# Feed-forward down projections on one Trainium2 core: eight block products of two k groups done as seven, shared ones added to the residual by VectorE

## What is computed

```python
def swiglu_2(x, w_in, w_out):                     # w_in 1024 x 5632, w_out 2816 x 1024
    gate, up = jnp.split(x @ w_in, 2, axis=-1)
    return (jax.nn.silu(gate) * up) @ w_out

def second_block(x, ...):
    h = x
    for i in range(2):
        h = layer_norm(DN_ALPHA * h + 0.5 * swiglu_2(h, ffn_w_in[i, 0], ffn_w_out[i, 0]), ...)   # a0, b0
        m = gla_mixer(h, ...) if i == 0 else retention_mixer(h, ...)
        h = layer_norm(DN_ALPHA * h + m, ...)
        h = layer_norm(DN_ALPHA * h + 0.5 * swiglu_2(h, ffn_w_in[i, 1], ffn_w_out[i, 1]), ...)   # a1, b1
    return h
```

## Time and profile before

| | |
|---|---|
| runs | median 1592.44 us (1590.9 to 1592.71, three runs) |
| the profiled execution | 1591.92 us, its span 1590.1 us |
| mean granted TensorE clock | 0.999 of full |
| TensorE matmul busy | 1580.2 us, 99% of the span |
| VectorE busy | 1118.8 us, 70% |
| ScalarE busy | 866.0 us, 54% |
| DMA | 341 MB, 215 GB/s on average |

### The profile page before, as it was taken

The page is one execution under the profiler, slowest core; times in us unless marked ns, Lnnn a source line. Parts: engine busy times, 40 slices in busy tenths (PEclk is TensorE's granted clock), DMA queues, the critical chain, the costliest instruction groups (busy, mean ns, idle before and its releaser), DMA issues.

```text
span 1590.1 us, 18691 instructions
## 1 busy us (share of the span) xinstructions
PE 1580.2 (99%) x7659; PEld 1317.9 (83%) x7659; DVE 1118.8 (70%) x1081; ACT 866.0 (54%) x907; POOL 105.0 (7%) x126
## 2 busy tenths in 40 slices
PE   9999999999999999999999999999999999999998
PEld 6888897788888888888988888888888998888886
DVE  6785566677875678865668886678856657688964
ACT  7564457556653766642655665366543435456650
POOL 0141000000000000001010000000000131000000
PEclk9999999999999999999999999999999999999999
DMA  8874463467854687562648765578545544587750
GB/s 339 247 237 190 179 245 133 159 252 231 282 181 172 263 280 265 177 240 96 238 159 310 232 225 213 224 229 287 211 185 196 192 172 152 189 292 233 242 212 27
DMA packets 51892, 341.38 MB, mean 215 GB/s; under 512 B 6240, under 2 KB 6624, under 8 KB 13408
## 3 DMA queue, kind: packets, MB, share of 16 engines
q1 hardware_dynamic: 44000, 301.94, 50.7%
q0 software_dynamic: 7584, 38.12, 10.8%
q10 hardware_dynamic: 224, 0.14, 0.0%
HBM read 339.12 MB, written 1.05 MB: 214 GB/s over the span
## 4 chain that ended last, share of the span: by engine, by line
PE 96%; DVE 2%; DMA 1%; ACT 1%; issue 0%; SPq 0%; DVEq 0%; ACTq 0%
PE bank L833 24%; PE bank L846 24%; PE bank L837 21%; PE bank L895 4%; PE bank L897 4%; PE bank L900 4%; PE bank L783 3%; PE bank L850 3%; PE bank L932 1%; PE bank L931 1%; PE bank L929 1%; DVE split L1876 1%; DMA h<-in_x 0%; DMA whole<-in_w_gla 0%; PE bank L1318 0%; PE bank L1108 0%
## 5 line engine op out<-in xcount | busy, mean ns | idle before, releaser
L1876 DVE TENSOR_TENSOR split<-whole,split 128x2048 fp32r<-128x2048 f32 (+2 forms) x329 | 704.4, 2161 | 203.8 <-ACT split L1436 202.1
L1436 ACT ACTIVATE split<-whole 128x2048 fp32r<-128x2048 f32 (+1 forms) x313 | 581.7, 1876 | 265.2 <-DVE whole L1880 38.7
L833 PE MATMUL bank<-split,xh 128*128 128x512 f32 x1052 | 288.1, 396 | 0.0
L846 PE MATMUL bank<-split,xh 128*128 128x512 f32 x1052 | 282.1, 390 | 0.0
L837 PE MATMUL bank<-split,xl 128*128 128x512 f32 x880 | 235.8, 390 | 0.0
L846 PEld LDWEIGHTS bank<-split,xh 128*128 128x128 f32 x1052 | 197.2, 188 | 41.8 <-DVE split L1876 0.4
L833 PEld LDWEIGHTS bank<-split,xh 128*128 128x128 f32 x1052 | 192.9, 188 | 40.7 <-issue 2.8
L837 PEld LDWEIGHTS bank<-split,xl 128*128 128x128 f32 x880 | 165.2, 188 | 35.4
L833 PE MATMUL bank<-split,th 128*128 128x512 f32 x524 | 143.7, 392 | 0.0
L837 PE MATMUL bank<-split,tl 128*128 128x512 f32 x524 | 142.2, 389 | 0.0
L846 PE MATMUL bank<-split,th 128*128 128x512 f32 x524 | 142.1, 389 | 0.0
(11 more groups left out here) (312 smaller groups left out, 1727.0 us busy)
## 6 DMA issues: line engine op xcount, KB each, us to landing
whole<-in_w_a_gate_up SPq DMA_DIRECT2D x48, 1024.0 KB, 7.4
whole<-in_w_b_gate_up SPq DMA_DIRECT2D x48, 1024.0 KB, 7.1
whole<-in_w_f_gate_up SPq DMA_DIRECT2D x45, 1024.0 KB, 7.1
whole<-in_w_ret SPq DMA_DIRECT2D x24, 1024.0 KB, 4.9
whole<-in_w_f_down SPq DMA_DIRECT2D x20, 1024.0 KB, 4.9
whole<-in_w_a_down SPq DMA_DIRECT2D x20, 1024.0 KB, 4.9
whole<-in_w_b_down SPq DMA_DIRECT2D x20, 1024.0 KB, 5.1
whole<-in_w_mix SPq DMA_DIRECT2D x16, 1024.0 KB, 4.9
```

The lines of the kernel that those rows point to most:

```text
L833: pe.matmul(o[:, :], tokens(0, k), whi[:, k, :], start=start and k == 0, stop=False, skip_group_check=True)
L846: ins = pe.matmul(o[:, :], tokens(0, k), wlo[:, k, :], start=False, stop=end, skip_group_check=True)
L1436: act.activation(split[s][:, 0:n], whole[r][:, 0:n], ACT.Copy).then_inc(hi.mark(i), 1)
L1876: dve.tensor_tensor(split[r][:, c0:c1], whole[r][:, c0:c1], split[s][:, c0:c1].bitcast(F32), ALU.subtract).then_inc(lo.mark(*what), 1)
```

## The change

In a0, a1, b0 and b1 the part of the down projection that is groups 2 and 3 (`UNIT_ROWS`) by both column halves and both token halves, eight block products, is done in seven. Their order is `DOWN_UNIT`. Two of the seven go straight into `ACC` (`b22`, `b21`), as does `t4`; `b11`, `t2` and `t3` accumulate one after the other in bank 0, `t1` stands in bank 1, and VectorE adds the state of those banks into the residual `h` each time (six additions, L2343 in the new file). `t2` may accumulate onto bank 0 only once the state after `b11` is added, and `t3` once that after `t2` is. ScalarE copies the transposed blocks of steps 3 to 6 a second time, unrounded, into the `gain` buffer (`ua`); VectorE makes four sums of them in `xn` (`us`) once turn 7 is done, ScalarE their high part in `xh`, VectorE the low part in `xl` (L2380). The gains are loaded only after those sums. The weights `t1` and `t3` get the adding second load, `t2` and `t4` a sum by VectorE (L2000 in the new file). The last four tiles are placed by fixed pairs, no longer the last eight. In GpSimd's queue the adding loads of down stand behind those of gate and up, and ahead of the layer's gains.

```diff
+DOWN_UNIT = (
+    ("tile", 0, 0), ("tile", 0, 1), ("turn", 10), ("blocks",), ("tile", 1, 0),
+    ("product", "b11"), ("product", "t1"), ("product", "b22"), ("product", "t2"), ("tile", 1, 1),
+    ("product", "t3"), ("product", "b21"), ("product", "t4"))
+UNIT_ROWS = (2, 3)
...
@@ plan_ffn
+            for step, *what in DOWN_UNIT:
...
+                    plan(key, {"b11": rows(p, 0), "b21": rows(q, 0), "b22": rows(q, 1),
+                               "t1": rows(p, 1), "t3": rows(p, 1)}.get(m), 4)
+                    if m in ("t1", "t3"):
+                        addend[i] = rows(p, 0) if m == "t1" else rows(q, 1)
...
@@ give_ffn
-            give_blocks(lead, end - 8, among)
-            if into_mixer:
+            give_blocks(lead, end - (4 if name in UNIT_IN else 8), among)
+            if name in UNIT_IN:
+                closing = [[s] for s in slots if into_mixer and s >= 5]
+                give_slots(end - 4, end, closing + [range(5) if into_mixer else slots] * (4 - len(closing)))
+            elif into_mixer:
...
@@ pool_program
-            for g in (7, 8):
-                pool_gain(pool, g)
-            for g in (9,):
-                pool_gain(pool, g)
+            pool_gain(pool, 7)
             pool_sums(pool, "a0")
+            for g in (8, 9):
+                pool_gain(pool, g, "a0")
...
@@ pe_unit
+            def product(m):
+                if m == "b11":
+                    pe.wait_ge(turn_lo.sem, turn_lo.of("t", name, max(range(3, 7), key=order.turned.index)))
+                    pe_product(pe, grp.b11, *block(0, grp.first), bank[0], True)
+                elif m == "t1":
+                    pe.wait_ge(fn.sem, fn.of("ush", name))
+                    pe.wait_ge(vec.sem, vec.of("usl", name))
+                    pe_product(pe, grp.t1, *sums(0), bank[1], True)
+                elif m == "t2":
+                    pe.wait_ge(vec.sem, vec.of("ud", name, 0, 0, "b11"))
+                    pe_product(pe, grp.t2, *sums(1), bank[0], False)
+                elif m == "b22":
+                    pe_product(pe, grp.b22, *sums(3), ACC[0][1], False)
+                elif m == "t3":
+                    pe.wait_ge(vec.sem, vec.of("ud", name, 0, 1, "t2"))
+                    pe_product(pe, grp.t3, *sums(2), bank[0], False)
+                elif m == "b21":
+                    pe_product(pe, grp.b21, *block(0, grp.second), ACC[0][0], False)
+                else:
+                    pe_product(pe, grp.t4, *block(1, grp.second), ACC[1][0], False)
...
@@ act_ffn, turn(j)
+                for m, k in unit_part(name, j):
...
+                    act.activation(ua[:, :, m, k:k + 2, :].rearrange("p t c n -> p c t n"),
...
@@ dve_unit
+            def add(t, n, b, sign, m):
+                hh = half(h[:, t, :], n)
+                dve.wait_ge(passed.sem, passed.of(spot[name + "d", 0, m], 1))
...
+                dve.scalar_tensor_tensor(hh, b[:, :], sign * e.scale / ALPHA, hh, ALU.mult, ALU.add).then_inc(
+                    vec.mark("ud", name, t, n, m), 1)
...
+            def product(m):
+                dve_lows(dve, behind(spot[name + "d", 0, m]))
+                if m == "b11":
+                    add(0, 0, bank[0], 1.0, m)
+                elif m == "t1":
+                    add(0, 1, bank[1], 1.0, m)
+                    add(1, 1, bank[1], 1.0, m)
+                elif m == "t2":
+                    add(0, 1, bank[0], -1.0, m)
+                elif m == "t3":
+                    add(1, 1, bank[0], -1.0, m)
+                    add(1, 0, bank[0], 1.0, m)
```

More of the change, by code:

```diff
@@ L383, in plan_ffn, with rows @@
                             grp.b11 - 0.9, grp.t2 + 0.5, grp.t1 - 0.1, grp.t2 - 0.1)
-            plan_rows(name + "d", A[f"w_{name}_down"], A[f"w_{name}_down_head"])
+            if name not in UNIT_IN:
+                plan_rows(name + "d", A[f"w_{name}_down"], A[f"w_{name}_down_head"])
+                return
+            full, head, key = A[f"w_{name}_down"], A[f"w_{name}_down_head"], name + "d"
+            def rows(g, n):
+                return full[g - 1, n] if g else head[n]
+            p, q = UNIT_ROWS
+            for step, *what in DOWN_UNIT:
+                if step == "tile":
+                    spot[(key, *what)] = len(tiles)
+                    plan(key, rows(*what), 4 if what[0] else 2)
+                elif step == "product":
+                    m, = what
+                    spot[key, 0, m] = i = len(tiles)
+                    product_of[i] = (key, 0, m)
+                    plan(key, {"b11": rows(p, 0), "b21": rows(q, 0), "b22": rows(q, 1),
+                               "t1": rows(p, 1), "t3": rows(p, 1)}.get(m), 4)
+                    if m in ("t1", "t3"):
+                        addend[i] = rows(p, 0) if m == "t1" else rows(q, 1)
+            grp = group[key, 0] = Group(p, q, *(spot[key, 0, m] for m in Group._fields[2:]))
+            load_key[grp.t1], load_key[grp.t3], load_key[grp.b22], load_key[grp.b21] = (
+                grp.b11 - 0.9, grp.t2 + 0.5, grp.t1 - 0.1, grp.t2 - 0.1)
+            for g in (4, 5):
+                for n in range(2):
+                    spot[key, g, n] = len(tiles)
+                    plan(key, rows(g, n), 4)
         w_mix, w_gla, w_ret = A["w_mix"], A["w_gla"], A["w_ret"]
@@ L1034, in pe_ffn @@
             groups = k_groups(22)
-            for g in range(4):
+            if name in UNIT_IN:
+                pe_unit(pe, f, turn)
+                dn = [None] * 8 + [spot[name + "d", g, n] for g in (4, 5) for n in range(2)]
+            for g in range(0 if name in UNIT_IN else 4):
                 for n in range(2):
@@ L1055, in pe_ffn, with pe_unit, block, sums @@
                         pe_pass(pe, dn[8 + n], T, groups[g][0], t, ACC[t][n % 2], False, g == 5)
+        def pe_unit(pe, f, turn):
+            order, name, T = ORDER[f.name], f.name, (f.th, f.tl)
+            groups, grp = k_groups(22), group[f.name + "d", 0]
+            def block(t, g):
+                return [lambda k, m=m: m[:, groups[g][0] + k, t * P:(t + 1) * P] for m in T]
+            def sums(s):
+                return [lambda k, m=m: m[:, s, k, :] for m in (ush, usl)]
+            def tile(g, n):
+                for t in range(2):
+                    if g == 0 and n == 1:
+                        pe.wait_ge(vec.sem, vec.of("mult", name, order.plain[-2], t))
+                    if n == 0 and t == 0:
+                        pe.wait_ge(turn_lo.sem, turn_lo.of("t", name, order.last_turned(2 * g)))
+                    pe_pass(pe, spot[name + "d", g, n], T, groups[g][0], t, ACC[t][n], g == 0, False)
+            def product(m):
[18 more added lines that the diff above has]
+                    pe_product(pe, grp.t4, *block(1, grp.second), ACC[1][0], False)
+            for step, *what in DOWN_UNIT:
+                if step == "tile":
+                    tile(*what)
+                elif step == "turn":
+                    turn(*what)
+                elif step == "product":
+                    product(*what)
         def pe_project(pe):
@@ L1632, in act_ffn @@
                     act.activation(ph[:, :, :], pf[:, :, :], ACT.Copy).then_inc(fn.mark("ph"), 1)
-            act_high(act, ahead(dn[1]))
-            turn(10)
-            act_high(act, dn[11])
+            if name in UNIT_IN:
+                for step, *what in DOWN_UNIT:
+                    if step == "tile":
+                        act_high(act, ahead(spot[(name + "d", *what)], 1))
+                    elif step == "product":
+                        act_high(act, ahead(spot[name + "d", 0, what[0]], 1))
+                    elif step == "turn":
+                        turn(*what)
+                    elif step == "blocks":
+                        act.wait_ge(vec.sem, vec.of("us", name, 3))
+                        act.wait_ge(passed.sem, passed.of(gu[-1], 1))
+                        act.activation(ush[:, :, :, :], us[:, :, :, :], ACT.Copy).then_inc(fn.mark("ush", name), 1)
+            else:
+                act_high(act, ahead(dn[1]))
+                turn(10)
+            act_high(act, dn[-1])
             act_edge(act, e)
```

75 lines of the change are left out of this document (62 added, 13 removed).

## The result

| | before | after |
|---|---|---|
| runs | median 1592.4 us (1590.9 to 1592.71, five) | median 1619.53 us (1616.56 to 1623.75, five) |
| ratio | | 1.0172, 95% interval 1.0161 to 1.0184 |
| the profiled execution | 1591.92 us, span 1590.1 | 1623.75 us, span 1621.9 |
| mean granted clock | 0.999 | 0.991 |

The changed kernel is 27 us slower. The direction and the range (1602 to 1621) hold; the forecast of 1610.5 is 9 us too low. The profiled execution happens to be the slowest of the five, 4.2 us above their median.

The account below looks back on a forecast made before the run. TensorE was taken to bound the kernel: 48 matmuls fewer (-10.9), waits for `b11`'s addition (+13.2), closing tiles (+9.3) and edges (+6.4) gave +18.0 on 1591.9; with the median 0.5 higher, 1610.5 us, range 1602 to 1621.

Parts of the forecast that it names:

- What bounds the kernel: TensorE multiplies in 99% of the span, so each matmul less saves its full spacing and each added wait costs its length.
- Work beside other work at nothing: Per layer, added ScalarE copies and splits, two adding loads on GpSimd and one load on SyncE were costed at nothing.
- The margin before D: D is a0's first down matmul after turn 7, at 678.57; `t1`'s adding load was to end about 2 us ahead.
- The wait for `b11`'s addition: Before `t2` in all four layers, TensorE waits 3.3 us for VectorE's queue: +13.2 us, up to +16.4.
- The closing tile and the edge: In a0 and b0, 4.6 us for the late closing load (+9.3) and 3.2 us before transposing `h` (+6.4).
- the clock falls: Rival: TensorE drops to the lower clock after each of eight waits, 1.6 us each, 13 in all: 1623; chance 0.10.
- the rivals within 0.2%: Closing loads in time, so only `b11`'s wait counts (1594.7, chance 0.05), and the change does nothing (0.02); together given as 0.06.
- The rival on the other side: No wait before `t2` and closing tiles found loaded, leaving only the matmul gain of 10.9 us: 1581.5; chance 0.03.

Follow-up runs that it names:

- e4: The kernel before, with 11 of 12 matmuls of one weight tile and token half left out in each of four layers (44 in all): 1580.92 us, ratio 0.9936.
- e9: The changed kernel with VectorE adding `b11` and `t2` ahead of later splits, both fixed pairs on the last two closing tiles, edge before mixer splits: 1581.43 us.
- e1: The changed kernel, with VectorE adding `b11` before the split of tile 1, half 1, not behind it: 1604.33 us, ratio 1.0082.
- e5: The changed kernel, with the fixed pair of block 13 on the last of the four closing tiles, not the second: 1608.39 us, ratio 1.0109.
- e6: The changed kernel, with VectorE doing the edge's first token half before splitting three mixer tiles in a0 and b0: 1612.99 us, ratio 1.0134.
- e3: The changed kernel, with ten matmuls on unused data put into TensorE's wait before `t2`: 1613.15 us, ratio 1.0135.
- e2: The changed kernel, with VectorE adding `b11` right after the low part of `b22`, ahead of `t4`'s weight sum and two splits: 1604.2 us, ratio 1.0081.
- e10: The changed kernel, with unused matmuls filling all eight waits: before `t2`, before the second closing tile and before the edge transposes: 1614.16 us, ratio 1.0140.

## Why the prediction was right and where it was wrong

**What bounds the kernel: right.** e4 gives 10.2 us for 44 matmuls, and every wait that an experiment took from TensorE came back in the time.

**Work beside other work at nothing: right in the end, with less cover than I said.** e9 has all of it, and comes out at -9.9 of the -10.9 that the matmuls alone are worth. But the loads were mis-sized: `t1`'s adding load takes 12.3 to 13.3 us in this place where I took the 10.0 of gate and up. The margin before D (about 2 us as I wrote, 2.7 by my own figures) was none: in a0 it was issued at 666.18 and landed at D + 1, and ScalarE's copy waited 0.2 us for it. The cover was that VectorE first reads it for the weight sum at 684.69, D + 6.3. The plain load issued beside it was late once (a1's 3.41 us).

**The wait for `b11`'s addition: right to 0.1 us** (3.20 against 3.3, in a0, b0 and b1; in a1, 2.10, since the lower clock level behind the 3.41 us wait held TensorE up and not VectorE). e1 ties it to the split ahead of the addition.

**The closing tile and the edge: right place and mechanism, sizes near.** 4.17 for the b0 closing wait, and 1.54 with 1.88 and the 0.4 of late low parts for a0, against 4.6 in each. The edge 2.88 and 2.02, against 3.2. Both are smaller where TensorE had already been held by the clock, and with the clock held up they come to 4.1 and 4.4, 3.0 and 4.3, the last with the late load in it. e5 and e6 show each cause alone.

**The step that failed** is the one not in the sum: that TensorE runs at 2.4 GHz behind each wait as before it. Forecast were 10.9 us less of busy time and 28.9 us of waits. Measured in the profiled execution are 4.4 us more of busy time and 27.3 us more of waits, 3.4 of them a1's odd one. So the waits came out near, and 15.3 us are missing in the busy time; e9, with the same 7611 matmuls and no such wait, is busy 15.8 us less than after. I put "the clock falls" among the rivals at 0.10, with 1.6 us for each of eight waits, 1623. The trace shows eight such stretches in the profiled execution (behind the four `t2` waits, both edges, b0's closing wait and a1's odd one; none behind the two short closing waits of a0). Their price was right: 1.3 to 1.6 us for one before `t2` (e3), 1.3 and 1.4 at after's two edges (13.36 and 13.43 against 12.07). What the rival had wrong is that each costs: the one behind b0's closing wait was taken up by the edge wait that follows.

The Trainium skill (TensorE: Matmul & The Clock Gate, section "Why this matters for your kernels"), which I had weighed, warns that an idle TensorE between bursts of matmuls goes back to half clock; this should have been in the forecast. The traces agree, though not wait by wait: the lower level stands behind all four `t2` waits of after and behind none of e1's, which are 1.0 us, but e5's `t2` wait of 3.19 us in a0 has none behind it. I gave it little since no row of before showed a fall in mid-program; but before had no mid-program wait of over 0.4 us either, so those rows could not speak on it.

**The sum again.** Forecast 1610.5; plus 5.1 to 6.4 for the four stretches before `t2`; plus 2.7 for those at the two edges; plus about 1 us for restarts at the upper level (the first group behind a wait 1.20, otherwise 1.07, with ten waits). That is an estimate of 1619 to 1621, against a median of 1619.53. What is left is smaller than the spread of after, 7 us, and stays open. The profiled execution, 1623.75, also has a1's odd wait with a stretch behind it; that it comes so near the rival's 1623 is in part luck, since the rival knew nothing of that wait and counted a stretch that cost nothing. A small slip stands in the chances: the rivals within 0.2% have 0.05 and 0.02, which is 0.07 and not 0.06.

**The rival on the other side**, that the gain comes through (0.03, decided by 3.3 us less work ahead of the addition), was a fair one in kind: e9 is that version, at 1581.43 against the 1581.5 that was worked out for it. That these agree to 0.1 us is luck: the kernel before measured 1591.28 beside e9, so the same sum gives 1580.4. The gain needed all three orders changed, and not more speed.

## What to carry to other kernels

Where an engine waits for one result of another engine with a strict queue, add up what stands ahead of that one instruction; the average busy share says nothing (VectorE was 74% busy in the slow version and 76% in the fast one). Put such an instruction as early as its input allows, splits for later tiles behind it, and a block that comes free last under the tile that is needed last; then look at the next place, since taking one wait away showed another of 1.2 us. And to each wait of some 3 us on TensorE add about 1.6 us of lower clock (eleven of the twelve such cases below had it), unless another wait follows soon whose end does not hang on TensorE: then that one takes it up.

## What was not expected of the hardware

- Of the twelve waits before `t2` in the profiles of after, e5 and e6 (eleven of 3.2 us, one of 2.10), eleven are followed by a lower clock level within the next twelve matmuls, one (e5, a0) is not. Waits of 1.0 to 1.6 us in the down stages are not followed by one in any profile here; of those between 1.8 and 2.9 us some are (2.88 in after, 1.80 in e2) and some are not (1.88 in after, 2.60 in e5). Whether a given wait is hit differs. The spread differs as well: 7 us over the five runs of after, up to 2.5 us for before in any round, 1.2 us for e9. That the one makes the other is not shown; the runs of after with a granted clock of 0.992 alone lie between 1616.56 and 1619.93.
- With ten small matmuls, 2.33 us in a wait of 3.35, no lower level stands behind any of e3's four `t2` waits. With nine, 2.12 us in a wait of 4.36, one stands behind b0's edge in e10.
- A 1 MB load of down takes a median of 6.9 us in the changed kernel and 4.9 before; the one in flight beside `t1`'s adding load took 6.3 us in b0 and 12.5 in a1, with the same bytes and the same order. That was not taken further.
